# Expert 0's token rows from one-hot matrix products instead of a gather, in a routed mixture-of-experts layer

## What is computed

```python
p_group = softmax(hf @ rg_w + rg_b)                 # 4 groups
g_prob, g_idx = lax.top_k(p_group, 1)               # top-1 group
sel = take_along_axis(e_logits, g_idx)              # its 4 experts
top_p, top_i = lax.top_k(softmax(sel), 2)           # top-2 of them
w = g_prob * top_p / sum(top_p)
for e in range(N_EXPERTS):
    y = (silu(h @ w_gate[e]) * (h @ w_up[e])) @ w_down[e]
    out = out + combine[:, e:e + 1] * y
```

## Time and profile before

| | |
|---|---|
| median of 3 runs | 553.96 us (551.9 to 554.74) |
| the profiled execution | 551.27 us, span 549.5 us |
| PE busy in the span | 535.5 us (97%) |
| DVE busy | 421.5 us (77%) |
| ACT busy | 353.6 us (64%) |
| POOL busy | 92.6 us (17%) |
| DMA | 144.03 MB, mean 262 GB/s |
| weight granules | 96 of 1024 KB, 15.5 to 18.0 us from issue to landing |

### The profile page before, as it was taken

How to read it: one execution, slowest core, us unless ns; L and a number is a source line. 1 busy time by engine, 2 the same in 40 slices (tenths; PEclk the granted TensorE clock), 3 DMA queues, 4 the chain that set the end, 5 groups by cost and what they waited for, 6 DMA issues and landing times.

```text
span 549.5 us, 7877 instructions
## 1 busy us (share of the span) xinstructions
PE 535.5 (97%) x2662; PEld 437.4 (80%) x2663; DVE 421.5 (77%) x580; ACT 353.6 (64%) x473; POOL 92.6 (17%) x113
## 2 busy tenths in 40 slices
PE   7999999999999999999999999999999999999995
PEld 4988777777877888877788888888888888888883
DVE  5654599555864753588989898988989898988996
ACT  5553664780326253355778978788778978788745
POOL 3260000000000000031412222022212222110620
PEclk9999999999999999999999999999999999999998
DMA  8999112323020237649999999999999999999996
GB/s 321 374 306 396 30 66 78 76 79 78 0 78 0 78 114 253 226 146 321 349 381 375 376 393 383 347 340 359 390 370 369 375 395 369 368 395 393 323 210 203
DMA packets 63821, 144.03 MB, mean 262 GB/s; under 512 B 3833, under 2 KB 13361, under 8 KB 63665
## 3 DMA queue, kind: packets, MB, share of 16 engines
q1 hardware_dynamic: 56528, 120.24, 61.9%
q0 software_dynamic: 7120, 22.90, 13.8%
q10 hardware_dynamic: 144, 0.52, 0.2%
HBM read 132.77 MB, written 14.30 MB: 268 GB/s over the span
## 4 chain that ended last, share of the span: by engine, by line
PE 88%; DVE 5%; ACT 2%; DMA 2%; issue 2%; POOL 0%; DVEq 0%; POOLq 0%
PE ps L1507 25%; PE ps L1509 24%; PE ps L1508 24%; PE ps L1514 7%; PE ps L1658 2%; PE ps L1644 2%; PE ps L1620 1%; PE ps L1590 1%; PE ps L1685 1%; DMA arena<-norm_g 1%; DMA arena<-h_dram,meta 1%; DVE lo_ring L1317 1%; PE ps L1911 1%; DVE act_lo L1027 1%; DVE res L1486 0%
## 5 line engine op out<-in xcount | busy, mean ns | idle before, releaser
L1317 DVE TENSOR_TENSOR lo_ring<-arena,hi_ring 128x2048 fp32r<-128x2048 f32 x94 | 213.9, 2289 | 26.8 <-ACT hi_ring L894 26.7
L1507 PE MATMUL ps<-hi_ring,act_hi 128*128 128x512 f32 x576 | 229.8, 399 | 1.5 <-DVE lo_ring L1317 1.1
L1509 PE MATMUL ps<-hi_ring,act_lo 128*128 128x512 f32 x576 | 224.9, 390 | 0.0
L1508 PE MATMUL ps<-lo_ring,act_hi 128*128 128x512 f32 x576 | 224.4, 390 | 0.0
L894 ACT ACTIVATE hi_ring<-arena 128x2048 fp32r<-128x2048 f32 x94 | 180.1, 1916 | 28.1 <-PE ps L1509 28.1
L1507 PEld LDWEIGHTS ps<-hi_ring,act_hi 128*128 128x128 f32 x576 | 108.2, 188 | 23.5 <-issue 2.4
L1509 PEld LDWEIGHTS ps<-hi_ring,act_lo 128*128 128x128 f32 x576 | 108.1, 188 | 23.3
L1508 PEld LDWEIGHTS ps<-lo_ring,act_hi 128*128 128x128 f32 x576 | 108.4, 188 | 21.0
L1017 DVE SCALAR_TENSOR_TENSOR lo_ring<-arena,over,hi_ring 128x512 fp32r<-128x512 f32 x40 | 29.3, 748 | 29.4 <-ACT hi_ring L709 29.2
L1027 DVE TENSOR_TENSOR act_lo<-ps,act_hi 128x512 fp32r<-128x512 f32 x56 | 36.7, 684 | 7.0 <-ACT act_hi L742 5.1
L600 POOL DMA_INDIRECT arena<-h_dram,gather_idx x14 | 34.6, 2473 | 24.0 <-issue 24.0
(11 more groups left out here) (239 smaller groups left out, 524.2 us busy)
## 6 DMA issues: line engine op xcount, KB each, us to landing
arena<-w_gate SPq DMA_DIRECT2D x32, 1024.0 KB, 16.7
arena<-w_up SPq DMA_DIRECT2D x32, 1024.0 KB, 18.0
arena<-w_down SPq DMA_DIRECT2D x32, 1024.0 KB, 15.5
arena<-w_in SPq DMA_DIRECT2D x16, 512.0 KB, 6.4
y_dram<-arena POOLq DMA_DIRECT2D x8, 512.0 KB, 10.7
res<-y_dram POOLq DMA_DIRECT2D x8, 512.0 KB, 9.7
arena<-w_in SPq DMA_DIRECT2D x2, 1024.0 KB, 11.0
arena<-w_out SPq DMA_DIRECT2D x4, 512.0 KB, 6.2
```

What stands on the lines that cost most here:

```text
L1317: nc.vector.tensor_tensor(lo(N1 + n12), raw(n12), hi(N1 + n12).bitcast(F32), ALU.subtract).then_inc(lo_done, 1)
L1507: nc.tensor.matmul(dst, a_hi, b_hi, start=start, stop=False)
L1508: nc.tensor.matmul(dst, a_hi, b_lo, start=False, stop=False)
L1509: return nc.tensor.matmul(dst, a_lo, b_hi, start=False, stop=stop)
```

## The change

The products of expert 0 no longer wait for a gather. VectorE finds, for each token tile, the place of each token in expert 0's list (`find_first`) and writes it as a one-hot matrix `first_hot`. TensorE multiplies the normed rows, which stay in SBUF in four homes of their own (`h2_home`), with it (`first_rows`, 8 groups of 4 matmuls of 128x128), which gives expert 0's rows already transposed in PSUM. `keep_clock` goes. All lists are made behind those products, and the weight lists behind the products of granules 0 and 1. Expert 0's gather goes; experts 1, 2 and 3 are gathered whole. The differences for the gate weights move from VectorE to GpSimd. Lengths, slots and flags move into VectorE's step 0, and the running sums of the flags into the branch for long lists. SyncE waits for granule 8 on the last write of `h2_dram`, and for granules 9 and 10 on the one-hot products. The two y buffers change places.

```diff
-        h2_buf = [region(O_XG, D), region(O_XG + D, D)]
+        x_rows = [region(O_XG, D), region(O_XG + D, D)]
+        h2_home = [region(O_BIAS, D), region(O_BIAS + D, D), x_rows[1], x_rows[0]]
+        first_hot = region(O_BIAS + 2 * D, T * P).rearrange("p (t s) -> p t s", t=T)
...
@@ SyncE
-                if n == RING2 - 4:
-                    sp.wait_ge(rows_in[0], 16)
+                if n == O_BIAS // GRAN - 1:
+                    sp.wait_ge(h2_out[T - 1], 16)
+                elif n == O_BIAS // GRAN:
+                    sp.wait_ge(x_turned, 1)
+                elif n == O_BIAS // GRAN + 1:
+                    sp.wait_ge(x_turned, 2)
...
@@ GpSimd
+            pool_done(nc.gpsimd.tensor_tensor(diff.rearrange("p t g j -> p (t g j)"), route[:, 704:768], route[:, 640:704], ALU.subtract))
+            pool_done(nc.gpsimd.tensor_tensor(diff, diff, lg[:, :, 1:, :], ALU.mult))
+            nc.gpsimd.tensor_tensor(g_exp, lg[:, :, 0, :], g_top.unsqueeze(2).to_broadcast([P, T, 4]),
+                                    ALU.subtract).then_inc(pool_step, 1)
+            for n in (8, 4, 2):
+                pool_done(nc.gpsimd.tensor_tensor(folded[:, :, 0:n], folded[:, :, 0:n], folded[:, :, n:2 * n], ALU.add))
+            nc.gpsimd.tensor_tensor(route[:, 864:868].unsqueeze(2), folded[:, :, 0:1], folded[:, :, 1:2], ALU.add).then_inc(gate_d, 1)
...
+            pool.wait_ge(x_turned, 2)
+            gather_whole(1)
+            gather_whole(2)
...
@@ ScalarE
             split(2, 2, 16)
-            rows_hi(0, 1)
+            nc.scalar.activation(stat[:, 46:47], eps[:, 0:1], ACT.Exp)
+            rows_hi(0, 1, (0,))
+            act.wait_ge(gate_d, 1)
+            nc.scalar.activation(route[:, 848:868], route[:, 848:868], ACT.Exp).then_inc(gate_e, 1)
+            rows_hi(0, 1, (1,))
+            nc.scalar.activation(stat[:, 47:48], eps[:, 0:1], ACT.Silu)
             split(3, 3, 16)
-            act.wait_ge(over_set, 1)
...
@@ VectorE
+            def find_first(t0, t1, ahead):
+                last = t1 == T
+                step_done(nc.vector.tensor_scalar(miss[:, t0:t1], standing[:, t0:t1, 0, 0], 2.0, 2.0 * S, ALU.is_ge, ALU.mult))
+                dve.wait_ge(rank_ready, 2 if last else 1)
+                step_done(nc.vector.tensor_tensor(first_rank[:, t0:t1], ahead, miss[:, t0:t1], ALU.add))
+                for t in range(t0, t1):
+                    nc.vector.tensor_scalar(first_hot[:, t, :], order, first_rank[:, t:t + 1], None,
+                                            ALU.is_equal).then_inc(first_hot_set, 1)
...
+            find_first(0, EARLY, ps[:, 1, 0:EARLY * E:E])
             find_ranks(0, EARLY, ps[:, 1, 0:EARLY * E])
-            mark(0)
             norm2(T - 1)
             gate(EARLY, T)
-            mark(1)
+            find_first(EARLY, T, ps[:, 2, 0:(T - EARLY) * E:E])
             find_ranks(EARLY, T, ps[:, 2, 0:(T - EARLY) * E])
-            for t in range(EARLY, T):
+            for t in range(T):
                 mark(t)
...
+            def step(b, e, last=False, first=False):
                 for c in range(PER_E):
+                    if c == 1 and first and b == 0:
+                        set_hid(e)
                     split(e * PER_E + 4 + c, (4 + PER_E * b + c) % RING2)
+                    if first and c == 0 and b == 0:
+                        rows_lo(1, 3)
+                    if first and c == 4 and b == 0:
+                        set_slots()
+                    if first and c == 5 and b == 0:
+                        set_flags()
+                    if c == 1 and not (first and b == 0):
+                        set_hid(e)
                     if c == 2:
                         row_lo(hid_t[1], 6, hid_t[0], hid_hi, e + 1, hid_lo)
+                        if first and b == 0:
+                            set_lengths()
...
@@ TensorE
-            keep_clock(3, 0)
+            def first_rows(t, a):
+                pe.wait_ge(h2_ready, t + 1)
+                pe.wait_ge(first_hot_set, t + 1)
+                for i in range(4):
+                    ins = nc.tensor.matmul(ps[:, 4 + a, i * P:(i + 1) * P], h2_home[t][:, row_cols(a, i)],
+                                           first_hot[:, t, :], start=(t == 0 and i == 0), stop=(t == T - 1 and i == 3),
+                                           skip_group_check=True)
+                return ins
+            first_rows(0, 0)
             logits(2 * T - 1)
-            keep_clock(2, 0)
+            first_rows(0, 1)
+            first_rows(1, 0)
...
             ins.then_inc(rank_ready, 1)
+            first_rows(1, 1)
+            for a in range(2):
+                first_rows(2, a)
+                first_rows(3, a).then_inc(x_turned, 1)
             pe.wait_ge(index_ready, 4)
-            for t in range(EARLY, T):
+            for t in range(T):
                 pe.wait_ge(onehot_ready, t + 1)
-                ins = list_fields(7, 0, t, False, t == T - 1)
+                ins = list_fields(7, 0, t, t == 0, t == T - 1)
             ins.then_inc(lists_made, 1)
-            keep_clock(21, 0)
```

More of the change, by code:

```diff
@@ L1391, in _, with set_lengths @@
-            nc.vector.tensor_copy(over[:, UNITS + 1:2 * UNITS + 1], flags[cur]).then_inc(over_set, 1)
-            def step(b, e, last=False):
+            def set_lengths():
+                step_done(nc.vector.tensor_scalar(quarters, count, float(QUARTER), None, ALU.is_gt))
+                for i in (2, 3):
+                    step_done(nc.vector.scalar_tensor_tensor(quarters, count, float(QUARTER * i), quarters,
+                                                             ALU.is_gt, ALU.add))
+                nc.vector.tensor_copy(meta_v[:, :, 3:4], quarters.unsqueeze(2)).then_inc(lengths_made, 1)
@@ new lines, in _, with set_flags @@
+            flags, any_flag = r(0, UNITS), r(64, 1)
+            def set_flags():
+                for i in range(1, S // P):
+                    ins = nc.vector.tensor_scalar(flags[:, (i - 1) * E:i * E], count, float(P * i), None, ALU.is_gt)
+                step_done(ins)
+                nc.vector.tensor_copy(over[:, 0:UNITS], flags)
+                step_done(nc.vector.tensor_reduce(any_flag, flags, AX_X, ALU.add))
+                nc.vector.tensor_copy(over[:, 2 * UNITS:2 * UNITS + 1], any_flag).then_inc(over_set, 1)
@@ new lines, in number_flags @@
+            def number_flags():
+                sums = [region(9 * GRAN + 64 * i, UNITS) for i in range(2)]
+                step_done(nc.vector.tensor_scalar(sums[0], over[:, 0:UNITS], 0.0, None, ALU.add))
+                for n in range(6):
+                    a, b = sums[n % 2], sums[1 - n % 2]
+                    nc.vector.tensor_copy(b[:, 0:1 << n], a[:, 0:1 << n])
+                    step_done(nc.vector.tensor_tensor(b[:, 1 << n:], a[:, 1 << n:], a[:, 0:UNITS - (1 << n)], ALU.add))
+                step_done(nc.vector.memset(over[:, UNITS:UNITS + 1], 0))
+                nc.vector.tensor_copy(over[:, UNITS + 1:2 * UNITS], sums[0][:, 0:UNITS - 1]).then_inc(over_set, 1)
@@ L1401, in step @@
                     if c == 2:
                         row_lo(hid_t[1], 6, hid_t[0], hid_hi, e + 1, hid_lo)
+                        if first and b == 0:
+                            set_lengths()
                     if c == 3 and not last:
                         rows_lo(b, e * 2 + 5)
-            split(3, 3)
-            rows_lo(1, 3)
-            with dve.Fori(0, E // 2 - 1) as q:
+            for e in range(2):
+                step(e, e, first=True)
+            with dve.Fori(1, E // 2 - 1) as q:
@@ L1866, in step @@
                     down_half(4, last_t, 1, *at(9))
-            pe.wait_ge(rows_in[0], 16)
-            for a in range(2):
-                turn(4 + a, [x_rows[0][:, (4 * a + i) * P:(4 * a + i + 1) * P] for i in range(4)]).then_inc(x_turned, 1)
+            pe.wait_ge(x_lo, 1)
+            product(0, xt[0], 0, 0, 0, True, False, first=True)
+            pe.wait_ge(x_lo, 2)
+            product(0, xt[0], 4, 1, 1, False, True)
             pe.wait_ge(weights_set, 2)
```

176 lines of the change are left out of this document (81 added, 95 removed).

## The result

| | before | changed |
|---|---|---|
| median of 5 runs each, same chip | 552.15 us (551.84 to 554.74) | 549.19 us (548.95 to 550.24) |
| the profiled execution | 551.27 us, span 549.5 | 550.24 us, span 548.5 |

The changed kernel takes 0.9938 of the time of before (95% interval 0.9914 to 0.9961): 3.0 us less. The forecast was a gain of 2.2 us, to 551.7. Of the 2.5 us between that and 549.19, 1.8 us are the starting point: I counted from a median of three runs, 553.96, and the five runs of the same kernel have 552.15. The other 0.8 us are gain that I did not forecast. The time lies inside the range, near its lower end, but I had put the most chance, 0.51, on "within 0.5%", and the kernel became faster by 0.6%. Both intervals leave out no change; both still hold a gain of just 0.5%.

A forecast was written before the change was run, and what follows sets the result against it. TensorE, busy 97% of the span, was taken as the bound, with experts a fixed block. Terms -3.9 + 1.0 + 0.9 - 1.1 + 1.0 gave -2.1, by granule 10 starts -2.2 us: 551.7 us predicted, range 549.0 to 554.8.

The forecast's parts named there:

- Term A: Start of granule 0: the gather leaves the path, one-hot products come onto it; 246.5 instead of 250.36, -3.9 us.
- Term B: List products for the weights move from before granule 0 to behind granule 1, still on TensorE's path: +1.0 us.
- The second half of the rows: Ahead of granule 1: GpSimd's seven-operation chain ends at 245.3 with 1.3 us to spare, so TensorE does not wait.
- Term C: Behind granule 2: expert 1's gather, issued among queued weights, lands at 256.7; TensorE waits, +0.9 us (0 to 1.7).
- The rule of the Trainium skill: Expert 1's gather: DMA engines alternate between queues, so it lands after 6.5 us, at 254.1, with no wait.
- Term D: Ahead of granule 4: the 1.12 us hole, blamed on VectorE's slots, flags and running sums, goes; -1.1 us in the sum.
- Term E: Granules 8, 9 and 10: VectorE's lengths, slots and flags return in step 0, so TensorE waits; +1.0 us together.
- The period: TensorE's time per expert after the first granules: stays 17.67 us, so the shift is kept.
- the ending: Lists of the last experts and the kernel's end: same code with y buffers exchanged, put at nothing.
- the gather in time: Rival, behind granule 2: expert 1's gather lands by 255.8, no wait; gain 3.1 us, or 3.6; chance 0.22.

The follow-up runs named there:

- the best version: Changed kernel with VectorE's lengths, slots and flags moved and granules 10 and 11 held until expert 1's gather landed; 547.53 us, 0.9916 of before.
- the placement alone: Changed kernel with only VectorE's leftover work moved: lengths ahead of expert 1's low rows, slots behind them, flags into expert 1's step; 547.84 us.

## Why the prediction was right or wrong

**Term A, right in kind, too small.** Granule 0 gained 4.37 us where I had 3.9. The one-hot groups cost what the retention's products said: 246.72 - 242.23 = 4.49 us for five, 0.90 each. The other two pieces were sized too large. The rank sums come only 0.1 us later from the mark, not 0.25, and the groups behind them start before their busy time ends: on the times of the kernel before, at 240.6 and not 240.9. The eight list products advance TensorE by 0.90 us (246.72 to 247.62). The 1.04 of the earlier trace rows is the busy time of a row of products, which goes on under the next one's start.

**Term B, right, with the same oversizing.** The weights' list took 253.98 - 253.17 = 0.81 us of the path, not 1.04. Granule 2 gained 3.56 us against my 2.8.

**The second half of the rows, right.** GpSimd's seven operations ran at 0.21 to 0.38 us each, 2.43 us together (I had up to 3.5), and ended at 245.31. ScalarE waited for TensorE at that point, not for them. My own margins there do not add up: 1.3 us of room over seven operations is used up at 0.69 us each, not 0.75, and at 1.0 us each granule 1 would have waited 2.2 us, not 1.7. In the POOL timeline:

```profile
242.88 0.31 POOL L587 TENSOR_TENSOR y<-y 128x64 f32<-128x64 f32 x1
243.26 0.32 POOL L588 TENSOR_TENSOR y<-y,over 128x64 f32<-128x64 f32 x1
243.66 0.21 POOL L589 TENSOR_TENSOR y<-over,y 128x16 f32<-128x16 f32 x1
243.84 1.13 POOL L594 TENSOR_TENSOR y<-y 128x32 f32<-128x32 f32 x3
245.05 0.26 POOL L595 TENSOR_TENSOR y<-y 128x4 f32<-128x4 f32 x1
```

**Term C, the mechanism right, the size off.** The gather was slowed by the loads, and where TensorE waited for it, it was in the place I named. It landed after 8.3 us, in the second profile 7.5, not 9.1. The wait was 0.5 us in one profile and none in the other, where I had 0.9; over five profiles none is the usual case. The price was taken from the median of steady-state gathers; this one was issued while the queue was still filling, the DMA share 0.83 in the window of 245 to 250 us, and four of the five landed faster than the fastest of those, 8.2. The rule of the Trainium skill that I had set beside it (the page "DMA: Bandwidth & Descriptors", taking turns between queues) gave 6.5 us by my estimate; with four granules queued expert 1's gather took 7.5 to 8.3 us, between the two, and with two queued 4.9 and 5.6 us. What the rule made of the wait, none at all, came nearer than my 0.9 us in four of the five profiles.

**Term D, the right sum from a wrong cause.** The hole went and gave 1.26 us (2.93 to 4.19). The 1.1 in my listed sum is the bracket of the earlier trace rows; my own starts, from a gain of 1.9 to one of 3.2, had 1.3. But the small work that I blamed was covered in the kernel before. The kernel with the sums moved kept the hole, the changed kernel with the order put back got it again. What I missed stood in the order on VectorE: the low rows of expert 1 wait for a turn that TensorE makes only behind granule 2, and in the kernel before the low part of granule 4 stood behind them.

**Term E, right.** 1.0 us, 0.8 of it by the start of granule 10 against the kernel before, in the three places named. From 261.25, where `hid` starts, VectorE works without a gap until the low part of granule 10 begins at 277.12; with 2.2 us for that part this is 18.07 us, where I had 18.15, against 17.67. The waits are shorter than the 0.3 to 0.6 us that I named, 0.16 to 0.28 us each, and the slower restarts make up the rest.

**The period, right; the ending, wrong.** The period is unchanged. I had put the ending at nothing; it gave back 0.9 us of 3.5 (0.9 of 3.8 in the second profile). The ScalarE row that begins the last norms is the place, here of the changed kernel:

```profile
534.79 1.28 ACT L749 ACT_TABLE_LOAD   x1 [1.85 <-issue]
```

Its idle time, which the profile puts down to issue, lies behind the branch on the number of long lists. It was 1.18 us before, 1.84 in the second profile, 0.91 in the best version, 1.90 with the placement alone and 1.72 in the kernel before without `keep_clock`, all with the same code there. So it moves by up to 1.0 us with things far away, and of the changed kernel's 3.5 us some 0.5 were lost there, the rest behind VectorE's last instruction. Why it moves was not tested and stays open.

**The sum.** By the start of granule 10 the gain is 3.4 us (3.9 in the second profile) against my 2.2: 0.5 more from term A, 0.2 from B, 0.3 (0.8) from C and 0.2 from E; term D gave what my starts had. The ending takes 0.9 back. So what failed is the size of the terms and not the path: A was 0.5 us too small because the start of the groups and the list products were taken too dear (1.04 us where they advance TensorE by 0.90), B cost 0.8 and not 1.0, C cost 0.5 or nothing and not 0.9, and the ending was put at nothing and cost 0.9. That the time came within 1 us of the forecast gain is in part luck, since the ending gave back most of what the terms before it had missed. The errors before the ending all had one sign, because I took most prices from the dearer of two readings. The probabilities inherited this: I gave "the gather in time" 0.22, though my own text had its landing at 247.6 + 8.2, just when it was needed.

## What to carry to other kernels

Replacing a gather on the path by products from rows that are still on the chip takes the latency off the path and keeps TensorE busy, so no filler is needed. The loads can start earlier too, but no run shows that this gained anything here: holding two of them back again cost nothing. Before blaming the work in front of a late instruction, look up what the instruction just ahead of it in program order waits for; work that is covered costs nothing as long as it stays covered, and an order that puts a long wait ahead of ready work costs that wait. Price a step on the path by the distance between starts and not by the row's busy time.

## What the runs showed of the hardware

- An idle of 1.12 us on TensorE left the granted clock at 1.00. One of 2.21 us was followed by some 3 us at 0.50; in those of 5.90 and 6.64 us the clock fell to 0.50 before the idle ended. The 2.21 us cost 1.7 us more in one granule, the 5.90 us 2.7 us by granule 1.
- A gather of 128 rows of 4 KB landed after 4.7 to 5.4 us into idle DMA engines, 4.9 to 5.6 with two 1 MB loads in the queue, and 7.5 to 9.3 with four, or in the steady flow behind them. The last write of `h2_dram`, 512 KB, landed after 2.9 to 3.2 us, 4.0 with one load let go ahead of it, and 7.1 with four.
